# A third group of seven block products in the second down projection, with two weight sums of the other groups added ahead

## What is computed

```
h2 = rms_norm(x, norm2_g)
x = x + (silu(h2 @ w_gate) * (h2 @ w_up)) @ w_down      # w_gate, w_up: 1024 x 2816, w_down: 2816 x 1024
```

## Time and profile before

| | us |
|---|---|
| median of three runs | 804.03 |
| lowest and highest of them | 802.47, 804.63 |
| the profiled execution | 802.98 |
| its span, first to last instruction | 801.5 |
| TensorE busy | 795.6 (99%) |
| VectorE busy | 625.1 (78%) |
| ScalarE busy | 457.2 (57%) |
| GpSimd busy | 90.7 (11%) |

### The profile page before, as it was taken

How to read it: one execution, slowest core, us unless ns; L and a number is a source line. 1 busy time by engine, 2 the same in 40 slices (tenths; PEclk the granted TensorE clock), 3 DMA queues, 4 the chain that set the end, 5 groups by cost and what they waited for, 6 DMA issues and landing times. The chain is left out here.

```text
span 801.5 us, 13178 instructions
## 1 busy us (share of the span) xinstructions
PE 795.6 (99%) x5164; PEld 696.8 (87%) x5164; DVE 625.1 (78%) x1035; ACT 457.2 (57%) x738; POOL 90.7 (11%) x77
## 2 busy tenths in 40 slices
PE   8999999999999999999999999999999999999998
PEld 6888888999898888899999998887778888888886
DVE  6888989785555766679999997486866898787977
ACT  6667677554535544456656563466665566555552
POOL 0001000010011302101101110011100333011100
PEclk9999999999999999999999999999999999999999
DMA  9654564557432555475687656464424666884331
GB/s 317 187 166 157 176 229 145 151 146 228 123 118 88 172 173 199 167 237 180 193 251 244 224 186 209 165 203 160 156 79 147 198 207 214 288 282 161 107 103 54
DMA packets 118125, 144.09 MB, mean 180 GB/s; under 512 B 11552, under 2 KB 86704, under 8 KB 117808
## 3 DMA queue, kind: packets, MB, share of 16 engines
q1 hardware_dynamic: 115616, 141.22, 54.7%
q10 hardware_dynamic: 2448, 2.03, 1.0%
HBM read 141.78 MB, written 1.46 MB: 179 GB/s over the span
## 5 line engine op out<-in xcount | busy, mean ns | idle before, releaser
L1754 DVE TENSOR_TENSOR panel_lo<-panel_raw,panel_hi 128x1024 fp32r<-128x1024 f32 x237 | 300.8, 1272 | 106.8 <-ACT panel_hi L1236 105.1
L652 PE MATMUL bank<-x_halves,panel_hi 128*128 128x256 f32 (+1 forms) x1536 | 367.0, 322 | 0.7 <-DVE x_halves L2222 0.7
L1236 ACT ACTIVATE panel_hi<-panel_raw 128x1024 fp32r<-128x1024 f32 (+1 forms) x239 | 252.2, 1057 | 152.9 <-PE bank L652 150.8
L652 PE MATMUL bank<-x_halves,panel_lo 128*128 128x256 f32 x1024 | 288.3, 282 | 0.0
L652 PEld LDWEIGHTS bank<-x_halves,panel_hi 128*128 128x128 f32 x1536 | 255.8, 190 | 23.3 <-issue 0.9
L652 PEld LDWEIGHTS bank<-x_halves,panel_lo 128*128 128x128 f32 x1024 | 195.0, 190 | 0.2
L652 PE MATMUL bank<-panel_hi,x_halves 128*128 128x512 f32 x384 | 122.1, 399 | 0.0
L652 PEld LDWEIGHTS bank<-panel_hi,x_halves 128*128 128x128 f32 x384 | 70.0, 188 | 14.4 <-DVE panel_lo L1754 0.6
L652 PE MATMUL bank<-panel_lo,x_halves 128*128 128x512 f32 x192 | 75.1, 391 | 0.0
L652 PE MATMUL bank<-panel_hi,act_hi 128*128 128x512 f32 x156 | 60.9, 390 | 0.2 <-DVE panel_lo L1754 0.2
L652 PE MATMUL bank<-panel_hi,act_lo 128*128 128x512 f32 x156 | 60.7, 389 | 0.0
(11 more groups left out here) (312 smaller groups left out, 1017.1 us busy)
## 6 DMA issues: line engine op xcount, KB each, us to landing
panel_raw<-in_w_in SPq DMA_DIRECT2D x35, 1024.0 KB, 5.3
panel_raw<-in_w_up SPq DMA_DIRECT2D x30, 1024.0 KB, 5.4
panel_raw<-in_w_down SPq DMA_DIRECT2D x16, 1024.0 KB, 5.0
panel_raw<-in_w_gate SPq DMA_DIRECT2D x10, 1024.0 KB, 5.4
panel_raw<-in_w_out SPq DMA_DIRECT2D x8, 1024.0 KB, 5.0
panel_raw<-in_w_in SPq DMA_DIRECT2D x11, 512.0 KB, 4.7
panel_raw<-in_w_branch_fox SPq DMA_DIRECT2D x4, 1024.0 KB, 5.0
panel_raw<-in_w_branch_gdn SPq DMA_DIRECT2D x4, 1024.0 KB, 5.0
```

The source lines that it names most:

```text
L652: return e.matmul(o, l, r, start=start, stop=stop, skip_group_check=True)
L1236: return e.activation(o, i_, ACT.Copy, scale=scale)
L1754: e.tensor_tensor(lo, raw_view(i, k0, kt), hi.bitcast(F32), ALU.subtract).then_inc(s_lo, 1)
```

## The change

The last two pairs of k tiles (9 and 10: `GROUPS` = 0, 4, 18) become a third group. The plain halves fall from 14 to 10, the block products rise from 14 to 21. The third group uses the block buffers of the first and is loaded when these have been split for the last time. In the first two groups t1 and t3 are no longer added behind a split: VectorE adds them at steps of the gate and up projections (`SUMS_FROM`), t1 into a buffer of its own, and t2 and t4 stay behind splits. In the third group all four are added behind splits. GpSimd makes the sums of activations for pairs 9 and 10 too, right behind their products; their split parts lie in a place that the gate and up projections read until their end, so that ScalarE waits for that.

```diff
-GROUPS = 2
-DOWN2_ORDER = [(8, 0), (8, 1), (12, 0), (12, 1), (16, 0), (20, 0), (16, 1), (20, 1)]
+GROUPS = (0, 4, 18)
+DOWN2_ORDER = [(8, 0), (8, 1), (12, 0), (16, 0), (12, 1), (16, 1)]
 BLOCKS = ("b11", "b12", "b21", "b22")
-GROUP_ORDER = [("b11", None, "b21", None, "b22", None, "t3", None, "t1", None, "t2", None, "t4", None),
-               ("b11", None, "b21", None, "b22", None, "t3", None, "t1", "t2", None, "t4", None, None)]
-ADDED_BEHIND = {"b11": "t1", "b21": "t3", "b22": "t2", "t3": "t4"}
+GROUP_ORDER = [("b11", None, "b21", "b22", None, "t3", "t1", None, "t2", "t4"),
+               ("b11", None, "b21", "b22", None, "t3", "t1", None, "t2", "t4"),
+               ("b11", None, "b21", None, "b22", "t3", "t1", "t2", "t4", None, None)]
+SUM_PAIRS = [k // 2 + i for k in GROUPS for i in range(2)]
+ADDED_BEHIND = [{"b22": "t2", "t3": "t4"}] * 2 + [{"b11": "t1", "b21": "t3", "b22": "t2", "t3": "t4"}]
...
-BLOCKS_FROM = [END["up2", 1, 4], END["up2", 1, 6]]
+BLOCKS_FROM = [END["up2", 1, 4], END["up2", 1, 6], BLOCK_AT[0, "t4"] - 2]
+SUMS_FROM = [END["up2", 1, 6], END["up2", 1, 8]]
...
             def ffn2_hi(j):
                 e.wait_ge(s_g_mul, j + 1)
                 copy(acth[:, 2 * j:2 * j + 2, :], f2_tanh[j % 4]).then_inc(s_g_hi, 1)
-                if j < 2 * GROUPS:
-                    e.wait_ge(s_sums, 3 * j + 3)
-                    copy(act_sums_hi[:, j], act_sums[j % 2]).then_inc(s_sums_hi, 1)
+                if j in SUM_PAIRS:
+                    i = SUM_PAIRS.index(j)
+                    e.wait_ge(s_sums, 3 * i + 3)
+                    if i >= 4:
+                        e.wait_ge(*product(("up2", 1, KF // 2 - 1)))
+                    copy(sums_of(act_sums_hi, i), act_sums[i % 2]).then_inc(s_sums_hi, 1)
...
+                for g in range(2):
+                    for t_, at_ in (("t1", 0), ("t3", 2)):
+                        if n == SUMS_FROM[g] + at_:
+                            add_block(g, t_)
...
                 if n - 1 in TAIL2_AT:
                     j = TAIL2_AT[n - 1]
                     ffn2_mul(j)
-                    if j < 2 * GROUPS:
+                    if j in SUM_PAIRS:
                         act2_sums(j)
...
-                for g in range(GROUPS):
-                    for at_, b in zip(range(0, 8, 2), ("b11", "b12", "b21", "b22")):
+                for g in range(3):
+                    for at_, b in zip(range(0, 8, 2) if g < 2 else (0, 0, 0, 0), ("b11", "b12", "b22", "b21")):
                         if n == BLOCKS_FROM[g] + at_:
-                            e.wait_ge(*emptied(("out2", 1, 1)))
-                            e.dma_start(block_view(block_raw[g][b]), block_rows(g, b)).then_inc(block_landed(g, b)[0], 16)
+                            if g < 2:
+                                e.wait_ge(*emptied(("out2", 1, 1)))
+                            else:
+                                e.wait_ge(s_lo, BLOCK_AT[0, {"b11": "b11", "b12": "t3", "b22": "t2", "b21": "t4"}[b]])
+                            e.dma_start(block_view(block_raw[g % 2][b]), block_rows(g, b)).then_inc(block_landed(g, b)[0], 16)
```

More of the change, by code:

```diff
@@ L83 @@
 DOWN_ORDER = [(k, c) for k in range(0, KF - 6, HALF) for c in range(2)] + [(k, c) for c in range(2) for k in (16, 20)]
[L90 to L91 removed]
+GROUPS = (0, 4, 18)
+DOWN2_ORDER = [(8, 0), (8, 1), (12, 0), (16, 0), (12, 1), (16, 1)]
 BLOCKS = ("b11", "b12", "b21", "b22")
[L93 to L95 removed]
+GROUP_ORDER = [("b11", None, "b21", "b22", None, "t3", "t1", None, "t2", "t4"),
[3 more added lines that the diff above has]
+ADDED_BEHIND = [{"b22": "t2", "t3": "t4"}] * 2 + [{"b11": "t1", "b21": "t3", "b22": "t2", "t3": "t4"}]
+ADDS = [(g, t) for g in range(2) for t in ("t1", "t3")] + [(g, t) for g in range(3) for t in ADDED_BEHIND[g].values()]
 BLOCK_BANK = {"b11": ("p1",), "b21": ("down2", 0, 0), "b22": ("down2", 1, 0), "t4": ("down2", 0, 1), "t1": ("p5",),
@@ L600, in block_view, with block_buffer @@
             return t_.rearrange("p (k c) -> p k c", c=WIDE)
-        KEPT_IN = {b: b for b in BLOCKS} | {"t1": "b11", "t3": "b12", "t2": "b22", "t4": "b21"}
-        OTHER = {"t1": "b12", "t3": "b22", "t2": "b11", "t4": "b22"}
-        ADDS = list(ADDED_BEHIND.values())
+        KEPT_IN = [{b: b for b in BLOCKS} | {"t1": "b11" if g == 2 else "t1", "t3": "b12", "t2": "b22", "t4": "b21"}
+                   for g in range(3)]
+        ADDENDS = {"t1": ("b11", "b12"), "t3": ("b12", "b22"), "t2": ("t1", "b22"), "t4": ("t2", "b21")}
+        def block_buffer(g, b):
+            return block_raw[g % 2][KEPT_IN[g][b]]
         def block_landed(g, b):
-            return s_block[g][int(b[1]) - 1], 32
+            return s_block[g % 2][int(b[1]) - 1], 32 * (g // 2 + 1)
         def block_added(g, b):
-            return s_block_add, len(ADDS) * g + ADDS.index(b) + 1
+            return s_block_add, ADDS.index((g, b)) + 1
         def block_ready(g, b):
@@ L682, in block_product @@
                     else:
-                        if ("sums", j) not in waited:
-                            waited.add(("sums", j))
-                            e.wait_ge(s_sums_lo, j + 1)
+                        if ("sums", i) not in waited:
+                            waited.add(("sums", i))
+                            e.wait_ge(s_sums_lo, i + 1)
                         which = {"t1": SUM_1, "t2": SUM_2, "t3": SUM_3, "b22": SUM_4}[b]
-                        xh, xl = (x_[:, j, which, :] for x_ in (act_sums_hi, act_sums_lo))
+                        xh, xl = (sums_of(x_, i)[:, which, :] for x_ in (act_sums_hi, act_sums_lo))
                     for m, (xx, ww) in enumerate(((xh, hi), (xl, hi), (xh, lo))):
@@ L1245, in split @@
                     e.wait_ge(s_half, n - 4)
-                    copy(whi[(n - 1) % 4], block_raw[g][KEPT_IN[b]]).then_inc(s_hi, 1)
+                    copy(whi[(n - 1) % 4], block_buffer(g, b)).then_inc(s_hi, 1)
                     return
@@ L1730, in vector_program, with add_block @@
         def vector_program(e):
-            def add_block(g, b, n):
-                t_ = ADDED_BEHIND[b]
-                to = block_raw[g][KEPT_IN[t_]]
-                e.wait_ge(*block_landed(g, OTHER[t_]))
-                e.wait_ge(s_lo, n)
-                if ADDS.index(t_):
-                    e.wait_ge(s_block_add, len(ADDS) * g + ADDS.index(t_))
-                e.tensor_tensor(to, to, block_raw[g][OTHER[t_]], ALU.add).then_inc(s_block_add, 1)
+            def add_block(g, t_, n=None):
+                one, other = ADDENDS[t_]
+                for b in (one, other):
+                    e.wait_ge(*block_ready(g, b))
+                if n:
+                    e.wait_ge(s_lo, n)
+                    if (g, t_) == ADDS[4]:
+                        e.wait_ge(s_block_add, 4)
+                e.tensor_tensor(block_buffer(g, t_), block_buffer(g, one), block_buffer(g, other), ALU.add) \
+                    .then_inc(s_block_add, 1)
             def split(n):
```

45 lines of the change are left out of this document (25 added, 20 removed).

## The result

The changed kernel took 807.91 us (median of 6 runs, 807.39 to 809.46), the kernel before beside it 803.96 (802.44 to 804.63). The ratio is 1.0056, 95% interval 1.0042 to 1.0071: slower by 3.95 us, inside the predicted range (808.2, range 805.2 to 811.2). In a later comparison the same kernel took 810.13 us (807.77 to 810.83), beside 802.51 before: 1.0096, interval 1.0080 to 1.0111.

A forecast was written before the change was run, and what follows sets the result against it. TensorE, busy 99% of the span, was taken as the bound, with VectorE also full early in the stage. Matmuls -1.36, early stall +3.4 and end +2.7 made +4.7 us: from 803.53 to 808.2 us, range 805.2 to 811.2.

The forecast's parts named there:

- Matmuls: Second down projection on TensorE: 246 matmuls instead of 252, at 0.227 us each, -1.36 us.
- Sums ahead: Gate and up projections: four VectorE additions (t1, t3 of the first two groups) fit into idle time, costing nothing.
- Loads: Third group's w_down blocks, loaded into the first group's buffers, land before ScalarE wants them: no cost.
- Early stall: Start of the down stage: activation sums made ahead of d8's split keep TensorE waiting 3.8 us, net +3.4.
- d1: First step of the second down projection's stage, later ones numbered d2, d3 and on; predicted to start at 740.88 us.
- theory that ScalarE stands in order: Before d8: ScalarE takes pair 10's sums ahead of d8's split, so the split waits for GpSimd's last sum.
- The end: From d21's start T: VectorE's unpaused run ends at T + 24.2, TensorE alone at T + 21.5, so +2.7 us.
- wait for p1: After d21: ScalarE may copy p1 only after VectorE's addition of it into h, at T + 4.4.
- One small sign: Expected in the profile after: about 1.3 us of TensorE waits near the third group's t1.
- The sum: Whole change: -1.36 + 3.4 + 2.7 = +4.7 us, giving 808.2 us.
- rival 4: At d8 and d9: the stall also costs TensorE clock, say 3 us more, 811.2 us; chance 0.09.
- third rival: Set up for the follow-up experiments: the clock is the cause of the slowdown; no size or chance given.

The follow-up runs named there:

- fifth run: The kernel before (two groups), with t1 and t3 added ahead in the up projection, t1 into a buffer of its own: 802.02 us, 0.9994 of the kernel before.
- first run: The changed kernel with GpSimd's sums of pairs 9 and 10 moved to d9 and d13, their split parts to d12 and d16: 803.93 us.
- second run: The changed kernel with only ScalarE's and VectorE's split parts of pairs 9 and 10 moved to d12 and d16: 804.95 us.
- runs 3: The changed kernel with ScalarE copying bank p1 ahead of VectorE's addition of it: 807.35 us, and 807.62 us when run again.
- fourth run: The changed kernel with sums and split parts of pairs 9 and 10 moved later and bank p1 copied ahead of VectorE's addition: 802.24 us.
- runs 9 and 10: The kernel of 8 with one row addition (minus_w into h) left out, output incomplete (801.39 us), or put onto ScalarE and GpSimd (802.43 us).
- 8: The kernel of the fourth run with the third group's t1 and t3 also added ahead, at d15 and d17, in buffers of their own: 802.18 us.
- all sums behind splits: The changed kernel's three groups and order, but with no weight sums added ahead, all behind splits in the down stage: 810.00 us.
- pair 10's sums after d7: The changed kernel with GpSimd starting pair 10's sums only when d7's matmuls are done: 811.84 us.

## Why the prediction was right, point by point

- **Matmuls, -1.36.** 5158 against 5164 on the page, at the same spacing.
- **Sums ahead, 0.** Right, by the fifth run: the cover was there.
- **Loads, 0.** Right. TensorE works 23.00 of 23.00 us from 757 to 780 in the full-clock execution, the stretch into which the third group's blocks come.
- **Early stall, +3.4 net.** Right, and by the way described. Put on a d1 at 740.39, which is 0.49 earlier than in the rows, the prediction has the silu at 746.5, the product at 747.2, the last sum's end at 753.4 and d8 at 756.4; measured are 746.52, 747.28, 753.43 and 756.35. The first run removes 3.68 in all, 3.29 more than the 0.39 of before. The theory that ScalarE stands in order is borne out by the second run, for 2.6 us of it, though that run moved VectorE's part too; the other 1.1 are the turns that VectorE takes with GpSimd's sums.
- **The end, +2.7.** Right. d21 starts at T = 779.60 by count (102 matmuls behind d8). The prediction has d25's low part at T + 6.0 and the end at T + 24.2, and measured are T + 5.99 and T + 24.21. The wait for p1 is part of it (1.7 us, runs 3 and 4), VectorE's run as such the rest: in the fourth run TensorE ends 1.75 us earlier after d1 than in the kernel before, but the stage only 0.69, so that 1.06 is left. That VectorE's run sets the end once both stalls are mended is shown by runs 9 and 10. One small sign was off: TensorE's wait near the third group's t1 is 0.84 us, not 1.3.
- **The sum.** 4.7 forecast for the stage and 4.68 measured between the two profiles at full clock.

Two things lie beside the sum and were not in it.

First, **the output's last writes**. From VectorE's end to the end of the span it is 1.9 us before and 2.2 after, some 0.3 more. The issues from 795 us on, of the kernel before (KB each, median us to landing):

```profile
out<-h ACTq DMA_DIRECT2D x1, 128.0 KB, 1.8
out<-h SPq DMA_DIRECT2D x1, 128.0 KB, 1.8
```

and of the changed one at full clock:

```profile
out<-h ACTq DMA_DIRECT2D x1, 128.0 KB, 2.2
out<-h SPq DMA_DIRECT2D x1, 128.0 KB, 2.2
```

As VectorE no longer pauses for TensorE ahead of its last addition, the last writes are issued closer behind the 256 KB ones: SyncE's last issue comes 2.10 us after the start of those, before 2.88. From VectorE's end to the span's end it is 2.2 to 2.3 us in each of the third-group kernels that I read for it (runs 1, 4, 8, 10 and the changed one), and 1.9 in both two-group kernels. That queueing is the reason is argued from the spacing, not tested.

Second, **the clock**, rival 4, whose chance was set too low and whose size was too high for most executions. The prediction gave it 0.09 and some 3 us. It came in five of ten executions of the changed kernel: two at 0.998 (808.97 and 809.46) and three at 0.996 (809.79 to 810.83), 1.2 to 3.1 us over the 807.77 of those at 1.0. In the profiled one it cost 1.43: the chain's 96 matmuls from d8 on took 23.50 us (first line), against 22.07 at full clock (second).

```profile
756.60 23.50 PE bank L664 x96
756.35 22.07 PE bank L664 x96
```

That the stall makes the fall likelier is shown by the runs that shorten or lengthen it; that it is not the only cause, by the second and third row:

| wait before d8 | executions | clock |
|---|---|---|
| none or 0.6 us (runs 1, 2, 4, 8 and the row sum on GpSimd) | 50 | 0.999 to 1.0 in all |
| none (two groups ahead, one row sum left out) | 22 | 0.999 to 1.0 in 19, 0.998 in three |
| 0.39 us (the kernel before, later comparisons) | 64 | 1.0 in 58, 0.998 in six |
| 2.35 us (the changed kernel) | 10 | 1.0 in five, 0.996 to 0.998 in five |
| 2.35 us (p1 copied first, both times) | 10 | 0.999 to 1.0 in two, 0.995 to 0.998 in eight |
| 2.33 us (all sums behind splits) | 4 | 1.0 in all |
| 4.85 us (pair 10's sums after d7) | 4 | 0.992 to 0.998 in all |

Without the stall it is 9 of 136 executions, and none below 0.998; with a wait of 2.3 us or more it is 17 of 28, down to 0.992. What falls in the nine was not traced; those of the kernel before took 803.8 to 804.7 us.

Why the same wait costs clock in one execution and not in the next stays open, and the four executions with 2.33 us that kept full clock fit no rule by the length of that wait alone. The place of the fall differs too: in the profiled changed kernel it came some 2 us into the wait, while in the second profile of p1 copied first d8 had been running for 1.3 us (from 756.11; the clock fell at about 757.4). The Trainium skill (TensorE: Matmul & The Clock Gate, "What's actually happening") says that the window over which the array's activity is watched runs freely and does not start anew with the kernel, so that the moment of a change of clock depends on where in it the work falls. By that rule one kernel could give both outcomes, as these ten executions do; no run here moved the wait against it.

Four of the six times of the kernel before in the first comparison lie between 803.89 and 804.63. If those were executions at 0.998 (their clock is not recorded), the first ratio is too small: at full clock the difference is 807.77 - 802.5 = 5.3 us. As it is there at full clock, the clock is not what makes the changed kernel slower, and the third rival falls. Of the 5.3 us the stage has 4.68, the writes some 0.3, and the rest, some 0.3, seems to lie outside the span: the time is 1.77 us above it in the changed kernel's full-clock execution and 1.48 in the profiled one of the kernel before. Why was not looked for. So the mechanism and the 4.7 were right, but that 808.2 came so near to 807.91 is luck in part: the prediction stood on a base of 803.53 us, 1.0 above the 802.5 of full clock, and this made up for what it had left out.

## What to carry to other kernels

An algorithm with fewer matmuls is paid for in work on other engines, and its price is where in their order that work stands: here 3.7 us for the sums of activations, which nobody needed before d25 and which were made ahead of the split for d8. Before such a step is put where its input is made, ask who stands behind it on each engine, and when its result is first read. A kernel that ends on TensorE with a fraction of a microsecond to spare on VectorE can lose a matmul saving at its end: after both mends TensorE ended 1.75 us earlier, the stage 0.69.

## What I had not expected of the hardware

- With a wait of 2.35 us on TensorE the clock fell in five of ten executions of the changed kernel, in the profiled one to 1.2 GHz for some 3 us. In 50 executions of kernels with 0.6 us or none in that place it did not, but in nine of 86 others without the stall the mean clock was 0.998.
- GpSimd's three sums take 0.72, 0.46 and 0.45 us with VectorE idle and 1.53, 1.32 and 0.79 beside its additions and subtractions of two inputs. One GpSimd addition of 1.51 us cost VectorE's row additions 1.04 us. The Trainium skill (SBUF — State Buffer, "Who interferes with whom") says that a VectorE instruction with two SBUF inputs contends with a GpSimd instruction that reads SBUF; the rows agree in that both sides grow.
